# Rotary half turn of two attention stages: from a TensorE matmul to transfers issued by GpSimd, with the cosine product on GpSimd and the softmax-weight step in another place of the order

## The chip, the cores and the metric

The kernel runs on one core of one Trainium2 chip. The metric is the device time of one launch in microseconds (us), the median over runs. TensorE (PE in the profile) does matmuls, VectorE (DVE) and ScalarE (ACT) do element-wise work and can read the matmul result banks (PSUM), GpSimd (POOL) does element-wise work on SBUF and can issue DMA transfers, and SyncE (SP) issues the transfers of the weights. Each engine runs its own instructions strictly in the order of the program; engines meet only at semaphores.

## The reference

Two transformer-like blocks run one after the other on a 256 x 1024 input in float32, 14 stages in all. Two of these stages (layers 0 and 3 of the second block) are differential attention, called A here. Cut to what matters:

```python
def apply_rope(x, cos, sin):                       # heads of 64 columns, halves of 32
    x1, x2 = jnp.split(x, 2, axis=-1)
    return jnp.concatenate([x1 * c - x2 * s, x2 * c + x1 * s], axis=-1)

def diff_attention(h, w_in, w_out, lam_params, subln_g, cos, sin, layer_idx):
    q, k, v = split(h @ w_in)                      # 1024 + 1024 + 1024 columns
    q, k = apply_rope(q, cos, sin), apply_rope(k, cos, sin)
    p = softmax(mask(q @ k.T * scale))             # 8 heads, each with two components
    wts = p[:, :, 0] - lam * p[:, :, 1]
    o = rms_norm(wts @ v, subln_g) * (1 - lam_init)
    return o @ w_out
```

## The kernel before

Activations lie with their feature on the partitions and the 256 tokens along the row. The weights of all 14 stages come as one stream of 1 MB pieces in a ring of three slots. For every piece SyncE issues the transfer into `w_raw` (line 537), ScalarE rounds it into a high part `w_hi` (`hi_ahead`, line 625), VectorE subtracts to get the low part `w_lo` (`lo_ahead`, line 1262), and TensorE multiplies three times per tile with these parts (lines 2222 to 2224). A float32-accurate product is the sum of the three.

Each A stage has 16 pieces: 12 of the input projection (`in0` to `in11`) and four of the output projection (`D0` to `D3`, each in four quarters). The order of all work in an attention stage is a list of tokens, `ATTENTION["A"]`. Every engine walks the same list and does its own share of a token:

- `inK`: TensorE projects piece K into one of three result banks. ScalarE first makes `w_hi` of piece K+2 and then copies the result of piece K to SBUF (`evacuate`, line 876; the buffer `raw_qk` holds two pairs of tiles). VectorE makes `w_lo` of piece K+2.
- `rotK`: the rotation of one pair of tiles, two tiles of queries or two of keys, 128 partitions x 512 columns. TensorE multiplies the raw tile by the signed permutation `turn` (`turn_pair`, line 2450), which swaps the 32-partition halves of each head and negates one of them, into the bank `MISC`. VectorE (`rotate`) multiplies the raw tile by the cosines (line 1665), the turned one by the sines (line 1668) and adds both (line 1682). Before `rot0` it scales the cosine and sine tables by the token's norm factor (lines 1657, 1658).
- `SU`: the scores of head U. TensorE (`scores`, lines 2484, 2485, 2489); then VectorE takes the row maxima (`masked`, lines 1734, 1743), then ScalarE the exponentials (`exponentials`, line 916).
- `NU`: VectorE turns the exponentials of head U into weights (`weights`, lines 1753, 1764, 1767, 1771).
- `TU`: TensorE transposes these weights (line 2559), ScalarE copies them out (line 926).
- `WU`: TensorE multiplies them with the values (`weigh`, lines 2535, 2536), ScalarE copies the result (line 882).

The scores of heads 0 and 1 need rotations 0 and 1, those of heads 2 and 3 need rotations 2 and 3, and so on. Scores of head U also wait for the exponentials of head U-1, since they use the same banks. The first part of the list before, on which every engine's order depends, is:

```
in0 in1 in2 rot0 in3 rot1 in4 S0 rot2 in5 S1 rot3 N0 in6 S2 T0 rot4 N1 in7 W0 S3 T1 rot5 N2 in8 W1 S4 T2 rot6
N3 in9 W2 S5 T3 rot7 N4 sq0 in10 W3 S6 T4 sum0 N5 ...
```

GpSimd builds masks at the start (line 588 ends that), issues 128 transfers of 512 KB for the modulation of the first block (line 595), which end with the mLSTM stage, and has one copy per head in the B stage (line 607). In the A stages it does nothing. Stage C has rotations too (`rot0` to `rot4`), by the same `turn` matmul.

Of the kernel before, what the change touches and what calls it, by code (L numbers as in the profile page):

```python
# [55 lines left out]
for _name, _rows in ROWS:  # L56
# [17 lines left out]
ATTENTION = {  # L74
    "A": """in0 in1 in2 rot0 in3 rot1 in4 S0 rot2 in5 S1 rot3 N0 in6 S2 T0 rot4 N1 in7 W0 S3 T1 rot5 N2 in8 W1 S4 T2 rot6
            N3 in9 W2 S5 T3 rot7 N4 sq0 in10 W3 S6 T4 sum0 N5 ln0 nrm0 sq1 in11 T5 sum1 W4 S7 N6 ln1 D0.0 W5 sq2 hi0 D0.1
            nrm1 T6 N7 D0.2 D0.3 lo0 sum2 W6 ln2 D1.0 D1.1 nrm2 T7 D1.2 D1.3 hi1 lo1 W7 sq3 D2.0 D2.1 sum3 ln3 nrm3
# [88 lines left out]
def build(nc, a, out, stages):  # L166
# [13 lines left out]
    with ExitStack() as ctx:  # L180
# [120 lines left out]
        x_loaded = sem("x_loaded")  # L301
        first_loaded = [sem(f"first_loaded{s}") for s in range(KT)]
        first_mod = sem("first_mod")
        x_scaled = sem("x_scaled")
        xr_T = sem("xr_T")
        c_rows_loaded = sem("c_rows_loaded")
# [3 lines left out]
        cols_ready = sem("cols_ready")  # L310
        xin_T = sem("xin_T")
        ada_loaded = [sem(f"ada_loaded{x}") for x in range(2)]
# [83 lines left out]
        nb_ready = sem("nb_ready")  # L396
        sph_ready = sem("sph_ready")
        spl_ready = sem("spl_ready")
# [107 lines left out]
        def _(sp):  # L506
# [3 lines left out]
            def first(kt):  # L510
                if kt >= FIRST_SLOTS:
                    sp.wait_ge(first_used, 2 * (kt - FIRST_SLOTS) + 2)
                sp.dma_start(first_w[:, kt % FIRST_SLOTS, :, :], a["first"][kt]).then_inc(first_loaded[kt], 16)

# [35 lines left out]
        def _(pool):  # L550
# [46 lines left out]

            for st in plan.steps:
                if st["key"][0] == "B":
                    for kind, u in sequence("B"):  # L600
                        if kind != "U":
                            continue
                        if u < 8:
                            pool.wait_ge(sp_ready, u + 1)
                            if u:
                                pool.wait_ge(r_ready, u)
                            pool.tensor_copy(sp_hi, sp).then_inc(sph_ready, 1)


        @block.scalar  # L610
        def _(act):
# [79 lines left out]
            def opening():  # L691
# [18 lines left out]
                for j in range(4):  # L710
                    act.wait_ge(xin_T, j + 1)
                    act.activation(xt_pair(j), PS[4 + j][:, :].rearrange("p (t n) -> p t n", t=2),
                                   ACT.Copy).then_inc(xt_ready, 2)
                for kt in range(KT):
                    if kt == KT - 2:
                        hi_ahead(2)
                    act.wait_ge(xr_T, kt // 2 + 1)
# [3 lines left out]
                    act.wait_ge(xin_T, 4)  # L721
                    act.activation(work[:, kt, :], acc(kt), ACT.Identity, bias=shift, scale=scale).then_inc(t_ready, 1)
# [521 lines left out]
        def _(dve):  # L1244
# [211 lines left out]
            def opening():  # L1456
# [5 lines left out]
                def total(kt, x):  # L1462
                    dve.wait_ge(first_loaded[kt], 16)
# [186 lines left out]
            def rotate(st, k):  # L1650
# [18 lines left out]
                chained()  # L1669
                if kind == "C":  # L1670
# [23 lines left out]
            def stick_unit(st, u):  # L1694
# [8 lines left out]
                if u < 8:  # L1703
# [14 lines left out]
                    ins.then_inc(nb_ready, 1)  # L1718
                    dve.wait_ge(sph_ready, u + 1)
                    if u:  # L1720
# [498 lines left out]
        def _(pe):  # L2219
# [215 lines left out]

            def turn_pair(st, k, units):

# [5 lines left out]
                if st["rots"] + k:  # L2443
                    pe.wait_ge(roped, st["rots"] + k)
                if kind == "A" and st["att"] + units:
                    pe.wait_ge(ot_ready, st["att"] + units)
                elif kind == "C":
                    pe.wait_ge(ot_ready, st["att"])
                m = MISC[:, 0:nt * T].rearrange("p (t n) -> p t n", t=nt)
# [71 lines left out]
            def weigh(st, u, rots):  # L2521
# [367 lines left out]

            def turn_rows(rows, first, done):  # L2890

                for kt in range(KT):
# [132 lines left out]
```

## Time and profile before

| | before |
|---|---|
| time, median of 3 runs | 2407.66 us (2404.53 to 2410.88) |
| time of the profiled execution | 2406.78 us |
| span of the profiled execution | 2404.7 us |
| TensorE busy | 2345.0 us (98%) |
| VectorE busy | 1718.7 us (71%) |
| ScalarE busy | 1192.0 us (50%) |
| GpSimd busy | 80.7 us (3%) |
| mean granted clock of TensorE | 0.997 |

The span runs from the first to the last instruction; the time of the execution has 2.1 us around it. Busy time is the union of an engine's instructions. The first A stage rotates and scores between 1191 and 1267 us, the second between 2105 and 2181 us. A timeline row gives the start, the busy time, the engine, the line, and in brackets how long the engine had been idle and on whom it waited.

### The profile page before, as it was taken

What the parts mean: (1) busy time and instruction counts of PE and PEld (TensorE: products, weight loads), DVE (VectorE), ACT (ScalarE), POOL (GpSimd) and SP (SyncE); (2) the same over time, 40 slices, a digit from 0 to 9 for tenths busy, and PEclk for the clock granted to TensorE, in tenths of its full rate; (3) what the DMA queues carried; (4) which work ended last, traced back from release to release, by engine and by line L of the source; (5) the groups of instructions that cost most, each with busy time, mean ns of one, the idle gap of its engine ahead of it and who ended that gap; (6) DMA issues with size and microseconds to landing.
All of it is one profiled execution on the core that took longest, in us unless ns stands there. A gap on an engine that the chain in (4) does not pass through costs nothing.

```text
span 2404.7 us, 46561 instructions
## 1 busy us (share of the span) xinstructions
PE 2345.0 (98%) x19290; PEld 2259.5 (94%) x19290; DVE 1718.7 (71%) x2260; ACT 1192.0 (50%) x1489; POOL 80.7 (3%) x163
## 2 busy tenths in 40 slices
PE   6999999999999999999999999999999999999999
PEld 6999988999999989999988999899997899988999
DVE  7888788777877867655677666676667666677665
ACT  5335865334434655433556435654345633546434
POOL 1110000010010000000000000000000000000000
PEclk9999999999999999999999999999999999999999
DMA  8987465787788433455433554436542355443652
GB/s 342 326 314 264 158 217 204 279 295 267 273 297 289 175 135 111 172 194 191 172 123 124 208 192 158 148 116 209 193 175 79 123 204 193 156 153 111 210 192 105
DMA packets 75561, 471.62 MB, mean 196 GB/s; under 512 B 8632, under 2 KB 9144, under 8 KB 26808
## 3 DMA queue, kind: packets, MB, share of 16 engines
q1 hardware_dynamic: 56288, 400.79, 46.5%
q0 software_dynamic: 18432, 67.12, 7.9%
q10 hardware_dynamic: 728, 2.14, 0.3%
q8 instruction: 80, 1.31, 0.2%
q14 instruction: 33, 0.27, 0.0%
HBM read 468.96 MB, written 1.05 MB: 195 GB/s over the span
## 4 chain that ended last, share of the span: by engine, by line
PE 80%; DVE 10%; ACT 4%; DMA 4%; issue 2%; POOL 0%; ACTq 0%; DVEq 0%; POOLq 0%
PE bank L2222 23%; PE bank L2223 23%; PE bank L2224 23%; DVE w_lo L1262 2%; DMA ada_wbuf<-in_ada 2%; PE bank L2228 2%; DVE ada_wbuf L1411 2%; PE bank L2233 2%; PE bank L2229 2%; DMA ARENA<-in_first 1%; ACT w_hi L625 1%; PE bank L2450 1%; PE bank L2484 1%; ACT ARENA L916 0%; DVE ARENA L1734 0%
## 5 line engine op out<-in xcount | busy, mean ns | idle before, releaser
L1262 DVE TENSOR_TENSOR w_lo<-w_raw,w_hi 128x2048 fp32r<-128x2048 f32 x371 | 848.9, 2289 | 319.9 <-ACT w_hi L625 319.1
L625 ACT ACTIVATE w_hi<-w_raw 128x2048 fp32r<-128x2048 f32 x371 | 708.9, 1914 | 508.4 <-PE bank L2224 493.3
L2222 PE MATMUL bank<-h_hi,w_hi 128*128 128x256 f32 x3376 | 944.2, 280 | 1.5 <-DVE w_lo L1262 1.5
L2224 PE MATMUL bank<-h_hi,w_lo 128*128 128x256 f32 x3376 | 935.8, 277 | 0.0
L2223 PE MATMUL bank<-h_lo,w_hi 128*128 128x256 f32 x3376 | 935.8, 277 | 0.0
L2222 PEld LDWEIGHTS bank<-h_hi,w_hi 128*128 128x128 f32 x3376 | 634.7, 188 | 8.3 <-issue 5.1
L2223 PEld LDWEIGHTS bank<-h_lo,w_hi 128*128 128x128 f32 x3376 | 634.8, 188 | 3.5 <-issue 3.3
L2224 PEld LDWEIGHTS bank<-h_hi,w_lo 128*128 128x128 f32 x3376 | 634.6, 188 | 0.0
L2222 PE MATMUL bank<-d_hi,w_hi 128*128 128x256 f32 x1920 | 536.3, 279 | 4.1 <-DVE d_lo L1639 4.0
L2224 PE MATMUL bank<-d_hi,w_lo 128*128 128x256 f32 x1920 | 532.2, 277 | 0.0
L2223 PE MATMUL bank<-d_lo,w_hi 128*128 128x256 f32 x1920 | 532.1, 277 | 0.0
L2222 PEld LDWEIGHTS bank<-d_hi,w_hi 128*128 128x128 f32 x1920 | 360.6, 188 | 7.7 <-DVE d_lo L1639 5.5
L2223 PEld LDWEIGHTS bank<-d_lo,w_hi 128*128 128x128 f32 x1920 | 360.6, 188 | 0.5 <-issue 0.5
L2224 PEld LDWEIGHTS bank<-d_hi,w_lo 128*128 128x128 f32 x1920 | 360.5, 188 | 0.0
L1411 DVE CUSTOM_DVE_ANT_0 ada_wbuf<-ada_wbuf,c_rows 128x1024 f32<-128x1024 f32 x128 | 155.7, 1219 | 31.1 <-DMA ada_wbuf<-in_ada 31.1
L2228 PE MATMUL bank<-h_hi,w_hi 128*128 128x256 f32 x440 | 111.7, 286 | 3.2 <-ACT h_hi L676 2.8
L816 ACT ACTIVATE gate_s<-gate_s 128x512 f32<-128x512 f32 x44 | 27.9, 633 | 170.6 <-DVE gate_s L1572 170.6
L2229 PE MATMUL bank<-h_hi,w_lo 128*128 128x256 f32 x440 | 109.3, 281 | 0.0
L595 POOL DMA_DIRECT2D ada_wbuf<-in_ada x128 | 67.8, 530 | 786.0 <-DVE ada_sum L1411 756.2
L2228 PEld LDWEIGHTS bank<-h_hi,w_hi 128*128 128x128 f32 x440 | 83.5, 190 | 9.4 <-issue 7.7
L789 ACT ACTIVATE gate_s<-bank 128x512 f32<-128x512 f32 x40 | 24.0, 600 | 137.1 <-PE bank L2224 134.8
L1593 DVE CAST d_hi<-hid 128x512 fp32r<-128x512 f32 x88 | 37.5, 426 | 73.8 <-PE bank L2224 73.3
(407 smaller groups left out, 2271.9 us busy)
## 6 DMA issues: line engine op xcount, KB each, us to landing
w_raw<-in_ws SPq DMA_DIRECT2D x371, 1024.0 KB, 4.8
ada_wbuf<-in_ada POOLq DMA_DIRECT2D x128, 512.0 KB, 5.3
ARENA<-in_first SPq DMA_DIRECT2D x8, 1024.0 KB, 19.8
work<-in_x SPq DMA_DIRECT2D x1, 1024.0 KB, 11.3
ARENA<-in_wax ACTq DMA_DIRECT2D x1, 1024.0 KB, 4.8
out_y<-ARENA SPq DMA_DIRECT2D x4, 256.0 KB, 2.2
ARENA<-in_wg ACTq DMA_DIRECT2D x1, 768.0 KB
c_rows<-in_c SPq DMA_DIRECT2D x1, 512.0 KB, 4.9
```

Of the source, the lines that this page charges most:

```text
L595: pool.dma_start(ada_w[:, x, :], a["ada"][2 * (piece - 8) + x]).then_inc(ada_loaded[x], 16)
L625: act.activation(w_hi[:, slot, :], w_raw[:, slot, :], ACT.Copy).then_inc(hi_ready, 1)
L816: act.activation(gate_s[:, :, :], gate_s[:, :, :], ACT.Silu).then_inc(silu_ready, 1)
L1262: dve.tensor_tensor(w_lo[:, s, :], w_raw[:, s, :], w_hi[:, s, :].bitcast(F32), ALU.subtract).then_inc(lo_ready, 1)
L1411: dve.tensor_tensor_reduce(out=w, in0=w, in1=c_rows[:, :], scale=1.0, scalar=0.0, op0=ALU.mult, op1=ALU.add, accum_out=dst).then_inc(ada_c ...
L1593: dve.tensor_copy(d_hi[:, buf, :, :], hid[:, :, :]).then_inc(dve_chain, 1)
L2222: pe.matmul(o, whi, xhi, start=start, stop=False, skip_group_check=True)
L2223: pe.matmul(o, whi, xlo, start=False, stop=False, skip_group_check=True)
L2224: return pe.matmul(o, wlo, xhi, start=False, stop=stop, skip_group_check=True)
L2228: pe.matmul(o, whi, xhi, start=start, stop=False, skip_group_check=True)
L2229: pe.matmul(o, wlo, xhi, start=False, stop=False, skip_group_check=True)
L2233: return pe.matmul(o, whi, xlo, start=False, stop=stop, skip_group_check=True)
```

## The change

In the A stages the half turn of a rotation is no longer a matmul. When ScalarE has copied a pair of tiles to SBUF, GpSimd issues four transfers of 32 partitions x 2 KB, which write the swapped halves into `rot_moved`, a buffer of two places that shares its memory with `sp_r` (of stage B). The sign is put into the scaled sine table with `half_sign`. The product with the cosines moves from VectorE to GpSimd, behind the four transfers of its own rotation and behind the wait for the rotation before it. VectorE waits for the 64 counts of its transfers (`moved`), multiplies by the sines, waits for GpSimd's product (`gpsimd_part`) and adds. Stage C keeps the matmul.

In the list of the A stages, `NU` no longer stands ahead of an `in` token but behind it, ahead of the following `rot`; `rotK` moves behind the next `in`; and `TU` comes ahead of the next `S`.

Several semaphores are merged to make room (`first_loaded` by slot, `xin_T` and `xr_T` into `rows_turned`, `sph_ready` into `gpsimd_part`), and four small memsets fill `half_sign` at the start.

```diff
 ATTENTION = {
-    "A": """in0 in1 in2 rot0 in3 rot1 in4 S0 rot2 in5 S1 rot3 N0 in6 S2 T0 rot4 N1 in7 W0 S3 T1 rot5 N2 in8 W1 S4 T2 rot6
-            N3 in9 W2 S5 T3 rot7 N4 sq0 in10 W3 S6 T4 sum0 N5 ln0 nrm0 sq1 in11 T5 sum1 W4 S7 N6 ln1 D0.0 W5 sq2 hi0 D0.1
+    "A": """in0 in1 in2 rot0 in3 rot1 in4 S0 in5 N0 rot2 S1 in6 T0 rot3 S2 in7 N1 rot4 W0 T1 S3 in8 N2 rot5 W1 T2 S4 in9 N3
+            rot6 W2 T3 S5 in10 N4 rot7 sq0 W3 T4 S6 sum0 N5 ln0 nrm0 sq1 in11 T5 sum1 W4 S7 N6 ln1 D0.0 W5 sq2 hi0 D0.1
...
+        rot_moved = sp_r[:, :, :].rearrange("p a c -> p (a c)")[:, 0:4 * T].bitcast(F32).rearrange(
+            "p (b t n) -> p b t n", b=2, t=2)
+        half_sign = sb("half_sign", [P, 1])
...
+            for q in range(4):
+                link(pool.memset(half_sign[32 * q:32 * q + 32, :], 1.0 if q % 2 else -1.0))
...
             for st in plan.steps:
+                if st["key"][0] == "A":
+                    pool.wait_ge(rope_ready, 3 + st["key"][1])
+                    for k in range(8):
+                        pool.wait_ge(proj_ready, st["evac"] + ROT_PIECE["A"][k] + 1)
+                        for q in range(4):
+                            pool.dma_start(rot_moved[32 * q:32 * q + 32, k % 2, :, :],
+                                           raw_part("A", k)[32 * (q ^ 1):32 * (q ^ 1) + 32, :, :]).then_inc(moved[k % 2], 16)
+                        if st["rots"] + k:
+                            pool.wait_ge(roped, st["rots"] + k)
+                        pool.tensor_tensor(rot_a, raw_part("A", k), cos_r.unsqueeze(1).broadcast_to([P, 2, T]),
+                                           ALU.mult).then_inc(gpsimd_part, 1)
...
-                    link(dve.tensor_tensor(cos_r, cos_t[:, :], rstd[:, :], ALU.mult))
-                    link(dve.tensor_tensor(sin_r, sin_t[:, :], rstd[:, :], ALU.mult))
+                    if kind == "A":
+                        dve.tensor_tensor(cos_r, cos_t[:, :], rstd[:, :], ALU.mult).then_inc(rope_ready, 1)
...
+                        link(dve.scalar_tensor_tensor(out=sin_r, in0=sin_t[:, :], scalar=half_sign[:, 0:1], in1=rstd[:, :],
+                                                      op0=ALU.mult, op1=ALU.mult))
...
-                link(dve.tensor_tensor(rot_a[:, 0:nt, :], raw_part(kind, k)[:, 0:nt, :], cosb, ALU.mult))
-                dve.wait_ge(turned, st["rots"] + k + 1)
-                m = MISC[:, 0:nt * T].rearrange("p (t n) -> p t n", t=nt)
+                if kind != "A":
+                    link(dve.tensor_tensor(rot_a[:, 0:nt, :], raw_part(kind, k)[:, 0:nt, :], cosb, ALU.mult))
+                if kind == "A":
+                    dve.wait_ge(moved[k % 2], 64 * (4 * st["key"][1] + k // 2 + 1))
+                    m = rot_moved[:, k % 2, :, :]
...
                 link(dve.tensor_tensor(rot_b[:, 0:nt, :], m, sinb, ALU.mult))
                 chained()
+                if kind == "A":
+                    dve.wait_ge(gpsimd_part, 16 * st["key"][1] + k + 1)
...
                 if kind == "A":
-                    pe.wait_ge(roped, st["rots"] + rots)
                     if u == 4:
...
                     elif step == "rot":
-                        turn_pair(st, k, outs if kind == "A" else 0)
+                        if kind == "C":
+                            turn_pair(st, k)
                         rots += 1
```

## Rows read from the trace of the kernel before

**Rows 1.** The page, its first part: busy time of each engine

```profile
PE 2345.0 (98%) x19290; PEld 2259.5 (94%) x19290; DVE 1718.7 (71%) x2260; ACT 1192.0 (50%) x1489; POOL 80.7 (3%) x163
```

**Rows 2.** Chain that ended last, 1228 to 1238 us (start, us, what)

```profile
1228.32 0.43 PE bank L2535 x2
1228.75 0.22 PE bank L2536 x2
1228.97 0.64 PE bank L2484 x4
1229.61 0.22 PE bank L2485 x4
1229.83 0.43 PE bank L2489 x2
1230.26 0.33 PE bank L2559 x3
1230.59 0.86 PE bank L2450 x2
...
1237.10 0.43 PE bank L2535 x2
```

**Rows 3.** Line 2450: its matmuls (x42; ns min/median/max, first and last start)

```profile
L2450 PE MATMUL bank<-ARENA,turn x42: 378/592/697, 1191.4 to 2162.3; 128*128 128x512 f32 x40, 128*128 128x256 f32 x2
```

**Rows 4.** Timeline of VectorE, 1205.9 to 1221 us, first A stage

```profile
1205.91 1.15 DVE L1734 TENSOR_REDUCE ARENA<-bank 128x1 f32<-128x256 f32 x4 [2.40 <-PE bank L2489]
...
1210.85 2.29 DVE L1262 TENSOR_TENSOR w_lo<-w_raw,w_hi 128x2048 fp32r<-128x2048 f32 x1 [1.66 <-ACT w_hi L625]
...
1215.58 0.68 DVE L1668 TENSOR_TENSOR ARENA<-bank,hid 128x512 f32<-128x512 f32 x1
...
1216.91 0.17 DVE L1753 RECIPROCAL ARENA<-ARENA 128x4 f32<-128x4 f32 x1
...
1218.65 2.29 DVE L1262 TENSOR_TENSOR w_lo<-w_raw,w_hi 128x2048 fp32r<-128x2048 f32 x1
1221.51 1.15 DVE L1734 TENSOR_REDUCE ARENA<-bank 128x1 f32<-128x256 f32 x4 [0.57 <-PE bank L2489]
```

**Rows 5.** Timeline of ScalarE, 1207 to 1211 us

```profile
1208.89 1.92 ACT L625 ACTIVATE w_hi<-w_raw 128x2048 fp32r<-128x2048 f32 x1
```

**Rows 6.** Timeline of VectorE at the seventh head (S6), first A stage

```profile
1256.60 1.15 DVE L1734 TENSOR_REDUCE ARENA<-bank 128x1 f32<-128x256 f32 x4 [0.59 <-PE bank L2489]
```

**Rows 7.** The same two points (S0, S6) of the second A stage

```profile
2120.02 1.15 DVE L1734 TENSOR_REDUCE ARENA<-bank 128x1 f32<-128x256 f32 x4 [2.41 <-PE bank L2489]
...
2170.52 1.15 DVE L1734 TENSOR_REDUCE ARENA<-bank 128x1 f32<-128x256 f32 x4 [0.60 <-PE bank L2489]
```

**Rows 8.** Timeline of VectorE around rotation 0, first A stage

```profile
1191.35 0.42 DVE L1657 TENSOR_TENSOR hid<-cos_t,rstd 128x256 f32<-128x256 f32 x1
...
1194.07 2.28 DVE L1262 TENSOR_TENSOR w_lo<-w_raw,w_hi 128x2048 fp32r<-128x2048 f32 x1
1196.27 0.69 DVE L1665 TENSOR_TENSOR ARENA<-ARENA,hid 128x512 f32<-128x512 f32 x1
```

**Rows 9.** Timeline of TensorE at rotation 0, first A stage

```profile
1191.38 0.67 PE L2450 MATMUL bank<-ARENA,turn 128*128 128x512 f32 x1 [0.59 <-ACT scrap L839]
```

**Rows 10.** Lines 595 and 607: GpSimd's transfers and its copies

```profile
L595 POOL DMA_DIRECT2D ada_wbuf<-in_ada x128: 527/528/689, 38.1 to 861.9; - x128
...
DMA to landing us min/median/max: 3.6/5.3/8.9
...
L607 POOL CAST sp_r<-ARENA x8: 824/830/840, 1516.2 to 1589.8; 128x768 fp32r<-128x768 f32 x8
```

**Rows 11.** The page, DMA issues (KB each, median us to landing)

```profile
out_y<-ARENA SPq DMA_DIRECT2D x4, 256.0 KB, 2.2
```

**Rows 12.** Windows in stage C: busy time of each engine, granted clock, DMA

```profile
1842.00:1844.00 2.00, 0.00 (x0) 0.00 (x1) 1.97 (x6) 1.93 (x9) 0.00 (x0) 0.98 1.00 426
1844.00:1846.00 2.00, 1.97 (x10) 1.67 (x11) 1.93 (x8) 0.00 (x0) 0.00 (x0) 0.50 0.03 8
1846.00:1848.00 2.00, 2.00 (x14) 1.44 (x12) 1.93 (x9) 1.87 (x10) 0.00 (x0) 0.66 0.00 0
```

**Rows 13.** Timeline of VectorE at the start of the kernel

```profile
19.00 1.23 DVE L1466 CUSTOM_DVE_ANT_0 ARENA<-ARENA,c_rows 128x1024 f32<-128x1024 f32 x1 [4.60 <-DMA ARENA<-in_first]
```

More of the change, by code:

```diff
@@ L301, in build @@
         x_loaded = sem("x_loaded")
-        first_loaded = [sem(f"first_loaded{s}") for s in range(KT)]
+        first_loaded = [sem(f"first_loaded{s}") for s in range(FIRST_SLOTS)]
         first_mod = sem("first_mod")
         x_scaled = sem("x_scaled")
-        xr_T = sem("xr_T")
         c_rows_loaded = sem("c_rows_loaded")
@@ L310, in build @@
         cols_ready = sem("cols_ready")
-        xin_T = sem("xin_T")
+        rows_turned = sem("rows_turned")
         ada_loaded = [sem(f"ada_loaded{x}") for x in range(2)]
@@ L389, in build @@
         turned = sem("turned")
+        moved = [sem(f"rope_moved{x}") for x in range(2)]
         roped = sem("roped")
@@ L396, in build @@
         nb_ready = sem("nb_ready")
-        sph_ready = sem("sph_ready")
+        gpsimd_part = sem("gpsimd_part")
         spl_ready = sem("spl_ready")
@@ L512, in first @@
                     sp.wait_ge(first_used, 2 * (kt - FIRST_SLOTS) + 2)
-                sp.dma_start(first_w[:, kt % FIRST_SLOTS, :, :], a["first"][kt]).then_inc(first_loaded[kt], 16)
+                sp.dma_start(first_w[:, kt % FIRST_SLOTS, :, :], a["first"][kt]).then_inc(first_loaded[kt % FIRST_SLOTS], 16)
             def weights(n):
@@ L606, in _ @@
                                 pool.wait_ge(r_ready, u)
-                            pool.tensor_copy(sp_hi, sp).then_inc(sph_ready, 1)
+                            pool.tensor_copy(sp_hi, sp).then_inc(gpsimd_part, 1)
         @block.scalar
@@ L710, in opening @@
                 for j in range(4):
-                    act.wait_ge(xin_T, j + 1)
+                    act.wait_ge(rows_turned, j + 1)
                     act.activation(xt_pair(j), PS[4 + j][:, :].rearrange("p (t n) -> p t n", t=2),
@@ L716, in opening @@
                         hi_ahead(2)
-                    act.wait_ge(xr_T, kt // 2 + 1)
+                    act.wait_ge(rows_turned, kt // 2 + 5)
                     act.wait_ge(first_mod, kt + 1)
@@ L720, in opening @@
                     act.activation(h_hi[:, kt, :], acc(kt), ACT.Identity, bias=shift, scale=scale).then_inc(hhi_ready, 1)
-                    act.wait_ge(xin_T, 4)
                     act.activation(work[:, kt, :], acc(kt), ACT.Identity, bias=shift, scale=scale).then_inc(t_ready, 1)
@@ L1462, in total @@
                 def total(kt, x):
-                    dve.wait_ge(first_loaded[kt], 16)
+                    dve.wait_ge(first_loaded[kt % FIRST_SLOTS], 16 * (kt // FIRST_SLOTS + 1))
                     w = first_w[:, kt % FIRST_SLOTS, x, :]
@@ L1656, in rotate @@
                     dve.wait_ge(rstd_ready, st["sq"] + 1)
-                    link(dve.tensor_tensor(cos_r, cos_t[:, :], rstd[:, :], ALU.mult))
-                    link(dve.tensor_tensor(sin_r, sin_t[:, :], rstd[:, :], ALU.mult))
+                    if kind == "A":
+                        dve.tensor_tensor(cos_r, cos_t[:, :], rstd[:, :], ALU.mult).then_inc(rope_ready, 1)
+                    else:
+                        link(dve.tensor_tensor(cos_r, cos_t[:, :], rstd[:, :], ALU.mult))
+                    if kind == "A":
+                        dve.wait_ge(masks_ready, 1)
+                        link(dve.scalar_tensor_tensor(out=sin_r, in0=sin_t[:, :], scalar=half_sign[:, 0:1], in1=rstd[:, :],
+                                                      op0=ALU.mult, op1=ALU.mult))
+                    else:
+                        link(dve.tensor_tensor(sin_r, sin_t[:, :], rstd[:, :], ALU.mult))
                     chained()
@@ L1664, in rotate @@
                 sinb = sin_r.unsqueeze(1).broadcast_to([P, nt, T])
-                link(dve.tensor_tensor(rot_a[:, 0:nt, :], raw_part(kind, k)[:, 0:nt, :], cosb, ALU.mult))
-                dve.wait_ge(turned, st["rots"] + k + 1)
-                m = MISC[:, 0:nt * T].rearrange("p (t n) -> p t n", t=nt)
+                if kind != "A":
[3 more added lines that the diff above has]
+                    m = rot_moved[:, k % 2, :, :]
+                else:
+                    dve.wait_ge(turned, k + 1)
+                    m = MISC[:, 0:nt * T].rearrange("p (t n) -> p t n", t=nt)
                 link(dve.tensor_tensor(rot_b[:, 0:nt, :], m, sinb, ALU.mult))
                 chained()
+                if kind == "A":
+                    dve.wait_ge(gpsimd_part, 16 * st["key"][1] + k + 1)
                 if kind == "C":
@@ L1718, in stick_unit @@
                     ins.then_inc(nb_ready, 1)
-                    dve.wait_ge(sph_ready, u + 1)
+                    dve.wait_ge(gpsimd_part, 8 + u + 1)
                     if u:
@@ L2434, in attention_input, with turn_pair @@
                     value_columns(st)
-            def turn_pair(st, k, units):
+            def turn_pair(st, k):
                 kind = st["key"][0]
@@ L2444, in turn_pair @@
                     pe.wait_ge(roped, st["rots"] + k)
[L2445 to L2448, printed above, removed]
+                pe.wait_ge(ot_ready, st["att"])
                 m = MISC[:, 0:nt * T].rearrange("p (t n) -> p t n", t=nt)
@@ L2888, in _, with turn_rows @@
             pe.wait_ge(cols_ready, ROW_TILES)
-            def turn_rows(rows, first, done):
+            def turn_rows(rows, first):
                 for kt in range(KT):
@@ L2896, in turn_rows @@
                     if kt % 2:
-                        last.then_inc(done, 1)
+                        last.then_inc(rows_turned, 1)
             pe.wait_ge(x_loaded, 16)
-            turn_rows(x_in, 4, xin_T)
+            turn_rows(x_in, 4)
             pe.wait_ge(x_scaled, TB)
-            turn_rows(x_rows, 0, xr_T)
+            turn_rows(x_rows, 0)
             pe.wait_ge(masks_ready, 1)
```

## The prediction, made before the changed kernel ran

> **What bounds the kernel now.** I read the page first. TensorE is busy for 98% of the span [rows 1], so the first guess for any change is: what TensorE no longer does comes off the time. That guess has to be tested where the change acts, so I took the chain of waits for one head in the first A stage [rows 2]. It holds nothing but TensorE: weigh 0.43 + 0.22, scores 0.64 + 0.22 + 0.43 = 1.29, transposes 0.33, the turn 0.86, and then a projection from 1231.45 to 1237.10, which is 5.65. One round of the order is 8.8 us and TensorE never waits in it.
>
> Then I read VectorE's timeline for the same work [rows 4], since the order list is walked by every engine. It idles, but its place in the order matters more than its busy time. From the maxima of S0 (1205.91) to the low part of the next piece (1210.85) are 4.94 us, of which 1.66 is a wait for ScalarE. ScalarE starts that high part at 1208.89 [rows 5], directly behind the exponentials of the same head. So there is a chain, maxima, exponentials, high part, low part, with no slack in it: low part k+2 starts 4.94 us after the maxima, whatever TensorE does. Before, this costs nothing, because only a later projection needs that low part, and the weights N were already made ahead of it.
>
> **What is taken off TensorE.** The turn matmuls of line 2450 are 42 records [rows 3], two to a rotation: 21 rotations, of which the five of stage C stay. 16 go, at 0.86 [rows 2]: 13.8 us. TensorE also idled 0.59 us before rotation 0, on a ScalarE copy which only the turn needed [rows 9]; twice that is 1.2. If TensorE stayed the bound, the time would fall by 15.0.
>
> **What the new order does to VectorE.** Its list now reads S3, in8, N2, rot5, S4. N2 is what transpose T2 waits for, and T2 stands ahead of S4 on TensorE. But VectorE gets to N2 only behind the low part of in8, and that ends the chain above. Counted from the start of the maxima of a head:
> - low part starts at 4.94 and gives the engine free 2.20 later (1194.07 to 1196.27) [rows 8]: 7.14
> - N takes 1.74 (1216.91 to 1218.65) [rows 4]: 8.88
> - T 0.33, scores 1.29 [rows 2] and 0.1 for the two hand-overs: maxima of the next head at 10.6.
>
> TensorE meanwhile has a projection and a weigh, 5.65 + 0.65 = 6.3, and waits 2.6. Every second head needs the rotation that stands between N and S as well: sine product and sum take 1.33 (1215.58 to 1216.91) [rows 4] against the 0.33 of T which they cover, so that round is 11.6. The four rounds from S2 to S6 take 10.6 + 11.6 + 10.6 + 11.6 = 44.4. Before they took 1256.60 - 1221.51 = 35.1 [rows 4, 6]. That adds 9.3.
>
> S0 to S2 is a special piece. On VectorE it reads S0, low 7, N0, rot2, S1, low 8, rot3, S2. N0 ends at 8.88, rot2 at 10.2, and only then come the maxima of S1, though TensorE had the scores at 6.9. Low 8 starts at 10.2 + 4.94 = 15.1 and ends at 17.35, rot3 at 18.7, S2 follows, and its maxima are at 20.1. Before it was 1221.51 - 1205.91 = 15.6 [rows 4]: 4.5 more. TensorE has in6 and T0 done at 12.9 and waits 5.8 us for rotation 3.
>
> Ahead of S0 something is won. TensorE enters in3 at 1190.8 instead of 1192.2 and has no second turn, so it reaches S0 2.3 us earlier. VectorE must keep up. The cosines are ready at 1191.8 [rows 8]; four issues at 0.53 [rows 10] start by 1193.4. For the landing of 64 KB between two SBUF places no row exists. Bounds: 2.2 us, a store of 256 KB [rows 11], and 8.9, the slowest of the 512 KB loads of the same queue [rows 10]. I take 3, as these are smaller than the fastest load with 3.6. Rotation 0 then ends at 1197.7, low 5 at 1199.9, rotation 1 at 1201.3, low 6 at 1203.5, just in time for the maxima at 1203.6. With 8.9 it would be 1209.4, which is 3.5 later than before instead of 2.3 earlier. Behind S6 the copy of the transposed weights has moved ahead of the exponentials: 0.4 less.
>
> Sum per A stage: -2.3 + 4.5 + 9.3 - 0.4 = +11.1. The second stage has the same distance from S0 to S6, 50.5 against 50.7 us [rows 4, 6, 7], so twice: +22.2.
>
> **The clock.** New idle time of TensorE is 5.8 once and 2.6 or more four times in each stage. In stage C the trace shows the engine without any matmul from 1842 to 1844 and the granted clock then at 0.50 for two us and 0.66 for the next two, that is at 1.2 instead of 2.4 GHz for some 3.3 us [rows 12]. Whether a fall hurts depends on where it falls: under a projection the wait covers it (6.3 + 1.7 is below 8.9), under T and S it lies on the chain and costs up to 0.33 + 1.29 = 1.6. Bounds per stage: 0, and 1.3 + 4 x 1.6 = 7.8. Between them I take half, 3.9, as the idle ends right before T and S but not each such pause need bring a fall. Twice: +7.8.
>
> **What lies beside other work.** The cosine product on GpSimd has no row; the copy of 768 columns takes 0.83 [rows 10], so 512 columns are at least 0.55, and I bound it at 1.4, twice VectorE's 0.69. It starts when the rotation before it is done and is needed at the next one, 8 us or more later, so it is covered; saved on VectorE are 0.61 per rotation that were not on the chain. The two-place buffer, the four transfers of a rotation (2.1 us of issue) and their landing lie in the same gap. DMA issues of the weight stream do not move in SP's queue. The sine table's other form (once per stage, some 0.1), and the waits dropped in `weigh`, cost nothing. The four memsets at the start, some 0.7 together with their waits, delay VectorE ahead of a 4.60 us wait for a transfer [rows 13] and vanish in it; without that cover they would cost 0.7. The merged semaphores count the same events in the same order.
>
> Two engines may still meet at a port. Product 1 starts when rotation 0 is done, which is when VectorE starts low 5; no row shows GpSimd computing beside VectorE there, so the sum holds nothing for it. The Trainium skill, page SBUF — State Buffer, section on the two separate sides, states that a VectorE instruction with two SBUF inputs and a GpSimd instruction that reads SBUF share a pair of ports which one of them holds for its whole length. By that rule product 1 and low 5 run one after the other and rotation 1 comes later by the product, about 1 us a stage, perhaps 2 with product 2 and low 6: 2439 to 2441 instead of 2437. No row before bears on it.
>
> **Rivals.**
> - *TensorE stays the bound.* It would be so if VectorE and ScalarE could run the weights N and the transfers' wait within TensorE's 7.9 us a round. Busy time speaks for it: VectorE has slack on the whole. Against it stand the two in-order engines and the 8.88. It decides if N is ready 6.3 us after the maxima. Time: 2406.8 - 15.0 = 2391.8.
> - *The transfers are the bound.* From the end of one rotation to the next pass product 1.0, the start of the fourth issue 1.6, the landing L and 1.33, so 3.9 + L, against the 8.5 (rotations 2 to 3) and 11.1 that the order leaves. It decides from a landing of about 5 to 7 us. At L = 8.9 each of seven gaps is 12.8: about 10 more behind S0 and 5.8 ahead of it per stage, 2406.8 + 22.2 + 32 = 2461. For it speaks that one GpSimd issue was seen to land after 8.9; against it that these are an eighth of that size and that no HBM is read.
> - *Gain and loss cancel*, by a shorter chain than I count, for which I see no row: within 7 us of 2407.
>
> **How the numbers follow.** The sum is made against the profiled execution, 2406.78 us, which lies 0.9 below the median of the runs, less than their spread: 2406.8 + 22.2 + 7.8 = 2436.8, so 2437. Without any clock fall it is 2429; 2425 if the rotation were also hidden in the two long rounds of each stage (1.0 each); less the 6.4 between the fastest and the slowest run, about 2420. With every fall on the chain it is 2445, and with the slowest landing ahead of S0 alone (5.8 a stage) 2456. Chances: this forecast 0.78, transfers as the bound 0.10, TensorE as the bound 0.09, cancelling 0.03. Range 2420 to 2456, which leaves out the fast rival, the cancelling and most of the transfer rival. A change of under 0.3% (7 us) is about what a measurement of this kernel cannot tell from none. Slower 0.88, same 0.03, faster 0.09.
>
> **What would show it.** After: no line 2450 in the A stages; in VectorE's timeline the order maxima, low part, reciprocal, with 4.94 between the first two and about 10.6 and 11.6 from maxima to maxima; TensorE waiting 2.6 or more for VectorE's line 1771 before each transpose, and about 6 for the sum of rotation 3; VectorE hardly waiting for transfers behind S0; granted clock below 1 in 1200 to 1260. The prediction is wrong if the maxima stand 8 us apart, or if VectorE's waits end on the DMA.

## The result and the profile after

The changed kernel takes 2445.03 us, median of 4 runs (2442.9 to 2448.81), against 2406.84 (2404.53 to 2410.88) for the kernel before: ratio 1.0156 [1.0142, 1.0169], 38 us slower. The forecast was 2437 in 2420 to 2456. The profiled execution took 2444.43 us with a span of 2442.7.

The page, busy time and chain by engine. TensorE's share fell from 98% [rows 1] although it does 32 matmuls less: it waits now. VectorE is 14% of the chain; before it was 10%.

```profile
PE 2349.8 (96%) x19258; PEld 2266.1 (93%) x19258; DVE 1711.6 (70%) x2244; ACT 1193.1 (49%) x1489; POOL 139.1 (6%) x247
...
PE 72%; DVE 14%; ACT 5%; issue 4%; DMA 4%; SPq 0%; POOL 0%; ACTq 0%; DVEq 0%
```

Line numbers have moved: maxima 1764 (before 1734), low part 1277 (1262), N 1783 to 1801 (1753 to 1771), sine product 1696, sum of the rotation 1712, scores 2511 to 2516, transpose T 2585. VectorE's timeline, first A stage (start, busy time, in brackets the idle time before it and what ended it):

```profile
1189.21 0.42 DVE L1673 TENSOR_TENSOR hid<-cos_t,rstd 128x256 f32<-128x256 f32 x1
1189.55 0.48 DVE L1678 SCALAR_TENSOR_TENSOR hid<-sin_t,half_sign,rstd 128x256 f32<-128x256 f32 x1
1196.47 0.69 DVE L1696 TENSOR_TENSOR ARENA<-sp_r,hid 128x512 f32<-128x512 f32 x1 [6.44 <-DMA sp_r<-ARENA]
1197.19 0.69 DVE L1712 TENSOR_TENSOR ARENA<-ARENA 128x512 f32<-128x512 f32 x1
1197.80 2.29 DVE L1277 TENSOR_TENSOR w_lo<-w_raw,w_hi 128x2048 fp32r<-128x2048 f32 x1
1200.01 1.75 DVE L1696 TENSOR_TENSOR ARENA<-sp_r,hid 128x512 f32<-128x512 f32 x1
...
1204.60 1.15 DVE L1764 TENSOR_REDUCE ARENA<-bank 128x1 f32<-128x256 f32 x4
...
1214.83 1.15 DVE L1764 TENSOR_REDUCE ARENA<-bank 128x1 f32<-128x256 f32 x4
...
1225.99 1.15 DVE L1764 TENSOR_REDUCE ARENA<-bank 128x1 f32<-128x256 f32 x4 [2.47 <-PE bank L2516]
...
1236.87 1.15 DVE L1764 TENSOR_REDUCE ARENA<-bank 128x1 f32<-128x256 f32 x4 [0.60 <-PE bank L2516]
1238.05 0.17 DVE L1773 TENSOR_SCALAR ARENA<-ARENA 128x4 f32<-128x4 f32 x1
1241.81 2.29 DVE L1277 TENSOR_TENSOR w_lo<-w_raw,w_hi 128x2048 fp32r<-128x2048 f32 x1 [3.59 <-ACT w_hi L641]
1244.02 0.17 DVE L1783 RECIPROCAL ARENA<-ARENA 128x4 f32<-128x4 f32 x1
...
1246.46 0.69 DVE L1712 TENSOR_TENSOR ARENA<-ARENA 128x512 f32<-128x512 f32 x1
1249.41 1.15 DVE L1764 TENSOR_REDUCE ARENA<-bank 128x1 f32<-128x256 f32 x4 [2.26 <-PE bank L2516]
```

This is the chain of the forecast: from the maxima at 1236.87 (S3) to the low part 4.94 us, of which VectorE idles 3.59 for the high part, then N, then the rotation, then the next maxima after 12.54. Before, the same two maxima (S3 and S4) stood 8.79 apart:

```profile
1230.30 1.15 DVE L1734 TENSOR_REDUCE ARENA<-bank 128x1 f32<-128x256 f32 x4 [1.18 <-PE bank L2489]
1239.09 1.15 DVE L1734 TENSOR_REDUCE ARENA<-bank 128x1 f32<-128x256 f32 x4 [1.17 <-PE bank L2489]
```

TensorE's side: its waits from 1188 to 1310 us (us in total, times, longest), and four rows of its timeline.

```profile
PE bank L2585 <- DVE ARENA L1801: 9.8, 4, 2.8
PE bank L2511 <- DVE ARENA L1712: 9.2, 4, 5.2
```

```profile
1202.54 0.73 PE L2511 MATMUL bank<-ARENA 64*128 64x256 f32 x4 [2.44 <-DVE ARENA L1712]
...
1223.57 1.23 PE L2511 MATMUL bank<-ARENA 64*128 64x256 f32 x4 [5.22 <-DVE ARENA L1712]
...
1234.99 0.55 PE L2585 MATMUL bank<-ident,ARENA 128*128 128x128 f32 x3 [2.21 <-DVE ARENA L1801]
1235.47 0.71 PE L2511 MATMUL bank<-ARENA 64*128 64x256 f32 x4
```

It waits 19 us in the stage: for N ahead of T1 to T4 (2.21, 2.74, 2.00 and 2.81), and for the rotation's sum ahead of S0, S2, S4 and S6 (2.44, 5.22, 0.78 and 0.78); in before's rows the score matmuls followed directly [rows 2]. The scores behind the long wait take 1.23 instead of 0.71. The windows say why (busy time and instruction count of PE, PEld, DVE, ACT, POOL, then the granted clock, the DMA share and GB/s):

```profile
1203.00:1205.00 2.00, 2.00 (x14) 1.76 (x11) 2.00 (x3) 0.00 (x0) 1.98 (x2) 0.53 0.95 369
1205.00:1207.00 2.00, 2.00 (x13) 2.00 (x12) 0.92 (x5) 1.01 (x5) 0.83 (x1) 0.62 0.60 152
1207.00:1208.00 1.00, 1.00 (x11) 1.00 (x10) 0.00 (x0) 1.00 (x6) 0.00 (x0) 1.00 1.05 442
...
1223.00:1224.00 1.00, 0.43 (x2) 0.43 (x4) 0.51 (x1) 0.00 (x0) 0.40 (x1) 0.79 1.17 164
1224.00:1226.00 2.00, 2.00 (x12) 1.61 (x11) 0.01 (x1) 0.00 (x0) 0.86 (x1) 0.50 0.80 336
...
1234.00:1236.00 2.00, 1.01 (x7) 0.82 (x9) 1.93 (x5) 0.42 (x1) 1.05 (x3) 1.00 0.92 193
```

After the waits of 2.44 and 5.22 us the engine runs at half clock (1.2 GHz) for some three us. After the 2.21 ahead of T1 it does not, nor after the 2.00 ahead of T3. Windows of 1 us show four such falls in each A stage: from 1203, 1223, 1247 and 1271, and at the same places of the second, where the one at S2 begins inside the long wait, at 2155, and lasts some seven us.

GpSimd's timeline ahead of S0, and the transfers' line (durations in ns, minimum/median/maximum):

```profile
1189.92 1.99 POOL L609 DMA_DIRECT2D sp_r<-ARENA  x4 [329.56 <-DVE hid L1673]
1191.93 1.30 POOL L613 TENSOR_TENSOR ARENA<-ARENA,hid 128x512 f32<-128x512 f32 x1
1193.17 2.00 POOL L609 DMA_DIRECT2D sp_r<-ARENA  x4
1197.97 3.24 POOL L613 TENSOR_TENSOR ARENA<-ARENA,hid 128x512 f32<-128x512 f32 x1 [2.80 <-DVE ARENA L1712]
```

```profile
L609 POOL DMA_DIRECT2D sp_r<-ARENA x64: 496/502/532, 1189.9 to 2193.3; - x64
...
DMA to landing us min/median/max: 1.8/4.8/6.3
```

The four issues end at 1191.9 and rotation 0 begins at 1196.47. VectorE stands still for 6.44 us. Queued behind it are low 5 (the low part of piece 5), rotation 1, which the scores of S0 need, and low 6, behind which the maxima of S0 stand. Product 1 (GpSimd's, of rotation 1) takes 3.24 beside low 5 instead of 1.30, and then sine product 1 takes 1.75 instead of 0.69.

Where the 38 us are, in us. A stage is counted from the instruction that makes `rstd` to the same of the next stage; maxima mark the heads. (The column without clock falls is e5 below.)

| part of an A stage | before | after | difference | e5 minus before | forecast |
|---|---|---|---|---|---|
| `rstd` to S0, first / second stage | 19.03 / 19.00 | 19.86 / 19.73 | +0.8 / +0.7 | +0.5 / +0.8 | -2.3 |
| S0 to S2 | 15.60 / 15.61 | 21.39 / 21.38 | +5.8 / +5.8 | +4.8 / +4.8 | +4.5 |
| S2 to S6 | 35.09 / 34.89 | 46.41 / 46.22 | +11.3 / +11.3 | +10.2 / +10.4 | +9.3 |
| S6 to the end | 41.03 / 40.94 | 41.87 / 42.06 | +0.8 / +1.1 | -0.2 / -0.2 | -0.4 |
| clock falls | | in the rows above | | 0 | +3.9 |
| stage | 110.75 / 110.44 | 129.53 / 129.39 | +18.8 / +18.95 | +15.1 / +15.7 | +15.0 |

Outside the two stages 2.1 us are won ahead of the first and 2.2 lost between them. I have no explanation for either that a run tests. Neither need be an effect of the change: the first `rstd` stands at 1186.88 before and 1184.74 after, and e1 to e5 and e8 to e12 spread from 1182.17 to 1190.47.

### The profile page after: what moved, and what is told of

It reads as the page before. It is cut to its first block, busy times and chain, and to the rows that moved or that the text cites. A ratio compares the mean times of both kernels' runs of the same rounds, so it can differ in the third digit from the quotient of the medians.

```text
span 2442.7 us, 46564 instructions
## 1 busy us (share of the span) xinstructions
PE 2349.8 (96%) x19258; PEld 2266.1 (93%) x19258; DVE 1711.6 (70%) x2244; ACT 1193.1 (49%) x1489; POOL 139.1 (6%) x247
## 4 chain that ended last, share of the span: by engine, by line
PE 72%; DVE 14%; ACT 5%; issue 4%; DMA 4%; SPq 0%; POOL 0%; ACTq 0%; DVEq 0%
PE bank L2252 21%; PE bank L2253 20%; PE bank L2254 20%; DVE w_lo L1277 4%; DMA ada_wbuf<-in_ada 3%; ACT w_hi L641 2%; DVE ada_wbuf L1426 2%; PE bank L2263 2%; PE bank L2258 1%; PE bank L2259 1%; ACT ARENA L931 1%; DVE ARENA L1764 1%; DMA ARENA<-in_first 1%; PE bank L2511 0%; DVE ARENA L1481 0%
## 5 line engine op out<-in xcount | busy, mean ns | idle before, releaser
L1426 DVE CUSTOM_DVE_ANT_0 ada_wbuf<-ada_wbuf,c_rows 128x1024 f32<-128x1024 f32 x128 | 155.8, 1221 | 30.4 <-DMA ada_wbuf<-in_ada 30.3
## 6 DMA issues: line engine op xcount, KB each, us to landing
work<-in_x SPq DMA_DIRECT2D x1, 1024.0 KB, 11.2
```

## Experiments

Theory O: the place of N behind the low part, with in-order engines, makes the loss. Rival T: the transfers and GpSimd's product make it. Rival K: it is the granted clock. Each ratio is to the kernel before.

| kernel | us, median | ratio, 95% interval | A stages, us |
|---|---|---|---|
| e1 order alone | 2450.25 | 1.0166 [1.0144, 1.0189] | 130.98 / 132.25 |
| e2 transfers alone | 2434.26 | 1.0099 [1.0078, 1.0121] | 124.59 / 123.50 |
| e3 N ahead again | 2428.66 | 1.008 [1.0059, 1.0102] | 121.23 / 122.10 |
| e4 no transfers | 2441.18 | 1.013 [1.0109, 1.015] | 126.68 / 126.78 |
| e5 waits filled | 2439.98 | 1.0137 [1.0118, 1.0157] | 125.89 / 126.17 |
| e6 issue on ScalarE, new order | 2418.85 | 1.0041 [1.0021, 1.0061] | |
| e7 as e6, product on VectorE | 2413.36 | 1.0023 [1.0011, 1.0035] | |
| e8 issue on GpSimd, new order | 2410.37 | 1.0014 [1.0003, 1.0025] | 112.16 / 108.98 |
| e9 as e8, issued early | 2402.03 | 0.9979 [0.9965, 0.9993] | 109.89 / 106.20 |
| e11 as e9, product on VectorE | 2403.29 | 0.9982 [0.9971, 0.9993] | 109.50 / 106.52 |
| e10 as e7, issued behind the factor | 2407.25 | 0.9999 [0.999, 1.0008] | 111.22 / 109.44 |
| e12 new order, turn on TensorE | 2429.93 | 1.0092 [1.0078, 1.0106] | 122.76 / 119.86 |

In e6 and e7 `rstd` itself comes later, so their stages can't be read by this measure. The stages are of one profiled execution each, and e8's is its fastest of ten, 2401.64 against a median of 2410.37: its stages stand for less than the median loses.

**e1, order alone.** The kernel before with its matmul and VectorE's product, and the changed list (W ahead of the rotation, since there they share a bank):

```diff
-    "A": """... S0 rot2 in5 S1 rot3 N0 in6 S2 T0 rot4 N1 in7 W0 S3 T1 rot5 N2 in8 W1 S4 ...
+    "A": """... S0 in5 N0 rot2 S1 in6 T0 rot3 S2 in7 N1 W0 rot4 T1 S3 in8 N2 W1 rot5 T2 S4 ...
```

> The kernel before with the new place of the weights N, of the rotations and of T ahead of S; the turn stays a matmul, the cosine product stays on VectorE, and weigh stands ahead of rot. Order theory (N behind the low part makes a chain maxima, exponentials, high part, low part, N, T, S): nearly all of the loss without any transfer. Rounds 10.8 and 12.2 us instead of 8.8, S0 to S2 about 21.3, so +16 us per A stage, 2434 to 2442 in all. Transfer theory (the landings make the loss): 2400 to 2412, since there are none.

Measured 2450.25, all of the loss, with 1.0166 against 1.0156, and 8 us above the range expected. The rounds (from maxima to maxima) are 10.8, 11.6, 11.2, 13.4, 10.9, 12.3 us. No transfer and no GpSimd product is in it, so T is not needed for a loss of this size. But the turn's bank and TensorE's matmuls for it are in it, and e12 will show that with another list they cost 22 us; e8 is free of them.

**e2, transfers alone.** The changed kernel with the list of before.

```diff
-    "A": """... S0 in5 N0 rot2 S1 in6 T0 rot3 S2 in7 N1 rot4 W0 T1 S3 ...
+    "A": """... S0 rot2 in5 S1 rot3 N0 in6 S2 T0 rot4 N1 in7 W0 S3 T1 ...
```

> The changed kernel with the order list of before: transfers and GpSimd product stay, N stands ahead of the low part again. Order theory: the loss goes, since the wait for a landing delays VectorE by a round but not the round itself; rounds 8.0 to 8.8, ahead of S0 +0.8: 2400 to 2416. Transfer theory: the landings now stand closer to the rotations and cost even more than in the changed kernel, 2445 or more.

Measured 2434.26: the expectation missed, and T's half of the story is real in this order. VectorE's timeline of e2, then GpSimd's:

```profile
1218.52 1.77 DVE L1773 TENSOR_SCALAR ARENA<-ARENA 128x4 f32<-128x4 f32 x1
1224.37 0.69 DVE L1696 TENSOR_TENSOR ARENA<-sp_r,hid 128x512 f32<-128x512 f32 x1 [4.08 <-ACT ARENA L891]
...
1228.93 2.29 DVE L1277 TENSOR_TENSOR w_lo<-w_raw,w_hi 128x2048 fp32r<-128x2048 f32 x1
1231.13 1.14 DVE L1764 TENSOR_REDUCE ARENA<-bank 128x1 f32<-128x256 f32 x4
```

```profile
1216.92 2.01 POOL L609 DMA_DIRECT2D sp_r<-ARENA  x4 [6.19 <-ACT ARENA L891]
1218.95 1.30 POOL L613 TENSOR_TENSOR ARENA<-ARENA,hid 128x512 f32<-128x512 f32 x1
```

In before's list rotation 3 stands directly behind S1. GpSimd issues its transfers from 1216.92, and they are in place only at 1224.4. The bracket names ScalarE's copy, but GpSimd had seen a copy of this line done at 1216.92; what VectorE waits for is the landing, 5.4 us behind the end of the last issue (the profile gives these four 5.2 to 5.8 from issue to landing). Behind it N0 and the low part wait. Of VectorE's sine products the profile puts 35.3 us of waits to the DMA in e2, 12.7 in the changed kernel. So the new order hides the transfers, and the place of N, chosen with it, costs more than they did.

**e3, N ahead again.** The changed kernel, every N one place up, ahead of `in`.

```diff
-    "A": """... S0 in5 N0 rot2 S1 in6 T0 rot3 S2 in7 N1 rot4 W0 T1 S3 in8 N2 ...
+    "A": """... S0 in5 rot2 S1 N0 in6 T0 rot3 S2 N1 in7 rot4 W0 T1 S3 N2 in8 ...
```

> The changed kernel with N alone moved ahead of the in token (S0 in5 rot2 S1 N0 in6 T0 rot3 S2 N1 in7 ...). Order theory: T no longer waits; rounds are 8.5 (bound by low part and rotation on VectorE) and 9.9 (scores wait for the rotation behind the low part) instead of 10.9 and 12.3, S0 to S2 18.4: about +5 us per stage against before, 2415 to 2422. Transfer theory: as the changed kernel, 2445.

Measured 2428.66, 7 us above the range expected. Moving N alone takes back 18 of the 38 us (by the ratios). The rest is in the rotations: TensorE waits 11.6 us of the first stage for their sum, which still stands behind the low part and right ahead of the scores. O was too narrow; not N alone, but N and the rotation behind the low part.

**e4, no transfers.** The changed kernel without the 64 transfers and without VectorE's wait for them. This leaves out the half turn: the sine product reads the unturned pair.

```diff
-                        for q in range(4):
-                            pool.dma_start(rot_moved[...], raw_part("A", k)[...]).then_inc(moved[k % 2], 16)
...
-                    dve.wait_ge(moved[k % 2], 64 * (4 * st["key"][1] + k // 2 + 1))
-                    m = rot_moved[:, k % 2, :, :]
+                    m = raw_part(kind, k)
```

> The changed kernel without the 64 transfers: VectorE takes the sine product of the raw tile itself, so the half turn is left out. Order theory: only the part ahead of S0 gets faster, 3 us per stage, and 2438 remains. Transfer theory: most of the loss goes, 2392 to 2410.

Measured 2441.18: without any transfer 31 of the 38 us remain (by the ratio), so the transfers are not the cause of most of it. GpSimd's product is still in it; e8 settles that. S0 now comes 16.7 us behind `rstd` in both stages, 2.3 earlier than before. That is the gain ahead of S0 which I had forecast and which the landing ate.

**e5, waits filled.** The changed kernel with unused 128x256 matmuls in TensorE's waits: ahead of S0 (4), S2 (12) and T1 to T4 (5 each).

```diff
+                    if kind == "A":
+                        for _ in range({("S", 0): 4, ("S", 2): 12, ("T", 1): 5, ...}.get((step, k), 0)):
+                            pe.matmul(PS[3][:, 0:T], ident[:, :], causal[:, 0:T], start=True, stop=True)
```

> The changed kernel with matmuls of no use in TensorE's waits: 4 ahead of S0, 12 ahead of S2, 5 ahead of each of T1 to T4, 0.46 us each, into a bank that nobody reads. If the fallen clock costs what I take it for (half-speed scores at S2, S4, S6: 1.3 + 0.9 + 0.5 and the tail of the stage 1.2), each stage gets 3 to 4 us shorter: 2437 to 2439, granted clock 1 throughout. If the clock costs nothing: 2445 or, by fillers that run over, 2446 to 2448.

Measured 2439.98 at a mean clock of 0.996 (0.992 without). More work, 5 us less time; the stages are 3.6 and 3.2 shorter. K is about a seventh of the loss by the medians and a fifth by the stages, as far as the filling itself costs nothing. With the clock up (no 1 us window from 1196 to 1296 or from 2112 to 2212 is under 0.97) a stage is still 15 us longer than before.

**e6, e7, e8, a new list.** If O holds in this wider form, a list that takes N and the rotations out from behind the low part, or leaves them a projection of time, must take the loss back. In these three N stands ahead of `in`, and so does every second rotation (3, 5, 7), so that no low part delays them:

```diff
-    "A": """... in4 S0 in5 N0 rot2 S1 in6 T0 rot3 S2 in7 N1 rot4 W0 T1 S3 in8 N2 rot5 W1 T2 S4 ...
+    "A": """... in4 S0 in5 rot2 S1 N0 rot3 in6 T0 S2 N1 in7 rot4 W0 T1 S3 N2 rot5 in8 W1 T2 S4 ...
```

e8 is that alone. In e6 ScalarE issues the transfers right behind its copy of the pair, and in e7 the product is on VectorE as well:

```diff
                 act.activation(dst, b, ACT.Copy, scale=0.125 if query else 1.0).then_inc(proj_ready, 1)
+                if kind == "A":
+                    act.wait_ge(proj_ready, st["evac"] + i + 1)
+                    for q in range(4):
+                        act.dma_start(rot_moved[...], dst[...]).then_inc(moved[rot % 2], 16)
```

> Transfers issued by ScalarE right behind its copy of the tile, the cosine product on GpSimd, and an order made for them: N and the odd rotation ahead of the low part, the even rotation behind it. Order theory: TensorE is nearly the bound again, rounds of 7.9, and the 13.8 us of turn matmuls mostly come off: 2392 to 2398. If transfers cost as such (issue time on ScalarE 4 x 0.45 us, landing of 4.8): 2400 to 2415.

> As e6, but the cosine product is back on VectorE and GpSimd has no part in the A stages. VectorE has 0.61 us more per rotation and rounds of 9.1 and 7.2: about 1 us per stage more than e6 if the two engines do not hold each other up; the same or less than e6 if GpSimd's product (1.28 alone, up to 3.24 beside a low part) costs VectorE as much. 2393 to 2400.

> The order of e6 with the transfers issued by GpSimd as in the changed kernel: tells what the issuing engine is worth. A GpSimd issue needs 2.0 us and lands after 4.8, so the odd rotation stands ready 7.3 us behind the projection instead of about 4; it holds the low part up by 2.4 in three rounds: 2403 to 2415. If the issuer doesn't matter: as e6.

Measured 2418.85, 2413.36 and 2410.37. e8 has every transfer and every product of the changed kernel and only another list, and takes back 34 of the 38 us: the loss is the list's, as O says. e6 and e7 miss (2392 to 2398 and 2393 to 2400 were expected), in part because of what else ScalarE has to do. Its timeline in e7:

```profile
1184.95 2.56 ACTq L884 DMA_DIRECT2D sp_r<-ARENA  x4
...
1188.19 2.44 ACTq L884 DMA_DIRECT2D sp_r<-ARENA  x4
1190.73 1.91 ACT L630 ACTIVATE w_hi<-w_raw 128x2048 fp32r<-128x2048 f32 x1 [2.57 <-issue]
1192.55 0.45 ACT L666 ACTIVATE lnb<-bank,eps_c 128x256 f32<-128x256 f32 x1
1193.04 0.42 ACT L668 ACTIVATE rstd<-lnb 128x256 f32<-128x256 f32 x1
```

Eight issues take 5.0 us and stand ahead of the norm factor, on which the cosines wait. From the start of the first pair's copy to `rstd` 8.7 us pass, in e8 3.3: the factor comes some 5 us later.

**e9, e10, e11, the start of the stage.** e8 leaves one wait ahead of S0, 6.07 us of VectorE for the landing. GpSimd issues only once the cosines exist, which only its product needs. e9 issues the first two rotations' transfers ahead of that wait; e11 also puts the product back on VectorE; e10 is e7 with ScalarE's first eight issues behind the norm factor.

```diff
+                    for k in (0, 1):
+                        pool.wait_ge(proj_ready, st["evac"] + ROT_PIECE["A"][k] + 1)
+                        for q in range(4):
+                            pool.dma_start(rot_moved[...], raw_part("A", k)[...]).then_inc(moved[k], 16)
                     pool.wait_ge(rope_ready, 3 + st["key"][1])
```

> As e8 (transfers from GpSimd in the mended order), but GpSimd issues the transfers of rotations 0 and 1 as soon as their pieces are evacuated, ahead of its wait for the cosines and of product 0. In e8's trace the pieces were evacuated by 1180 and the first issue started at 1187.35; VectorE waited 6.07 us for the landing ahead of rotation 0, and TensorE 2.1 us for rotation 1 ahead of S0. If the landing behind the cosines is what still costs time ahead of S0: that VectorE wait is gone or under 1 us, TensorE reaches S0 without a wait, and each A stage is about 2 us shorter, 4 us in all: 2404 to 2408. If e8's remaining loss lies elsewhere (clock, stage C): no change from e8's 2410.

> As e9, but the cosine product is back on VectorE, so that GpSimd only issues transfers. VectorE has 0.6 us more to do in every rotation; on the other side the low part and the sine product no longer meet a GpSimd product (1.75 us instead of 0.69 in e8's trace ahead of S0). If TensorE is the bound behind S0, both hide: within 2 us of e9. If VectorE's chain is the bound, 16 x 0.6 = 10 us slower than e9, less 2 x 1.1 us.

> As e7 (transfers issued by ScalarE, product on VectorE, mended order), but the eight issues of rotations 0 and 1 stand behind the norm factor on ScalarE instead of ahead of it. In e7's trace these eight took 5.0 us between 1184.95 and 1190.63 and the norm factor came at 1193.04. If they were e7's loss ahead of S0: the norm factor comes some 5 us sooner, each stage gets 3 to 6 us shorter, 2402 to 2408. If the issues only move their cost (the first rotation waits for them instead): about e7's 2413.

e9 takes 2402.03, ratio 0.9979 [0.9965, 0.9993]: 5 us faster than the kernel before, and 2 below the range expected. Only e9 and e11 beat it. VectorE's timeline of e9:

```profile
1189.48 0.48 DVE L1683 SCALAR_TENSOR_TENSOR hid<-sin_t,half_sign,rstd 128x256 f32<-128x256 f32 x1
1189.99 1.67 DVE L1701 TENSOR_TENSOR ARENA<-sp_r,hid 128x512 f32<-128x512 f32 x1
...
1201.37 1.15 DVE L1769 TENSOR_REDUCE ARENA<-bank 128x1 f32<-128x256 f32 x4 [1.55 <-PE bank L2521]
```

Rotation 0 follows the sines at once, and S0 comes 16.7 us behind `rstd`, as in e4: ahead of S0 the landing is fully covered. e11 is equal to e9 within the intervals, so the cosine product on GpSimd buys nothing here. e10 comes to 2407.25, 6 us better than e7, as expected. The place of the eight issues is so 6 us of e7's miss; what keeps e10 above the 2393 to 2400 once expected of e7 is open.

**e12, the new list without the transfers.** The kernel before with the list of e8.

```diff
-    "A": """... in4 S0 rot2 in5 S1 rot3 N0 in6 S2 T0 rot4 N1 in7 W0 S3 T1 rot5 N2 in8 W1 S4 ...
+    "A": """... in4 S0 in5 rot2 S1 N0 rot3 in6 T0 S2 N1 in7 rot4 W0 T1 S3 N2 rot5 in8 W1 T2 S4 ...
```

> The kernel before, turn matmul and VectorE product kept, with the mended order of e6 to e9. If that order alone brings something, this is as fast as e8 or e9 (2402 to 2410) and the transfers are worth nothing. If TensorE is the bound in this order as in the order of before, the same matmuls take the same time: 2404 to 2411, no change from before beyond 0.3%, and the 5 us that e9 wins come from the turns taken off TensorE. If the turn, now ahead of the low part, makes TensorE wait for rotations (as it did in e1 for up to 5.4 us): 2415 or more.

Measured 2429.93, the third of the three answers. TensorE's timeline of e12, then VectorE's:

```profile
1234.23 1.19 PE L2535 MATMUL bank<-ARENA 128*128 128x256 f32 x2 [2.83 <-DVE ARENA L1682]
```

```profile
1233.39 0.69 DVE L1682 TENSOR_TENSOR ARENA<-ARENA 128x512 f32<-128x512 f32 x1
```

With the turn in the bank that `weigh` writes, W0 has to wait until VectorE has read the turn. This list is good only because the turn has left the bank, and the list of before only because it has not. So e9's gain is no gain of the list alone.

## Why the prediction was right, and its steps

**What bounds the work** (right). The loss is the in-order chain maxima, exponentials, high part, low part, N. The low part starts 4.94 us after the maxima, as in the forecast, and e8 removes 34 of the 38 us by the list alone. N is ready 8.95 us after the maxima at 1225.99, against 8.88.

**S2 to S6, +9.3** (right, short by 0.9 to 1.1). With the clock held up (e5) the rounds of the first stage are 10.9, 11.75, 10.9, 11.7 against 10.6, 11.6, 10.6, 11.6. The hand-overs are dearer than my 0.1: from the start of the transpose to the maxima 1.88 us in the rows above, against 1.62 + 0.1.

**S0 to S2, +4.5** (right). +4.8 in e5. The forecast wait of 5.8 for rotation 3 is 5.22.

**Behind S6, -0.4** (right in size without the falls, -0.2).

**Ahead of S0, -2.3** (wrong, measured +0.8): the step that failed. Two sizes were off in it. I took the landing as 3 us "as these are smaller than the fastest load with 3.6"; the four of rotation 0 took 4.8 to 5.3, and rotation 0 begins 6.8 us behind the cosines instead of 4.6. Smaller did not mean faster. And the sum held nothing for two engines at a port, where 1.1 us went in sine product 1. The 2.2 and the 1.1 account, within 0.2, for the 3.1 by which the term was wrong. By the Trainium skill, page SBUF — State Buffer, section on the two separate sides, a VectorE instruction with two SBUF inputs and a GpSimd instruction that reads SBUF exclude each other. The trace agrees: product 1 starts at 1197.97 inside low 5 (1197.80 to 1200.09) and lasts 3.24 instead of 1.30, ending at 1201.21, and the sine product that meets it lasts 1.75. e4, without transfers but with the same meeting (sine products of 1.67 and 1.79), still reaches S0 2.3 earlier than before. So the meeting alone is covered there, and the landing is what uncovered it.

**The clock, +3.9 a stage** (right, 3.6 and 3.2 in e5 as the whole difference). The kind was off: I let all pauses count by half. Four falls a stage came, after the pause ahead of S0, and at S2, S4 and S6; none at the 2.21 us ahead of T1 or the 2.00 ahead of T3. Their cost is mostly where half speed meets scores on the chain: the scores at 1223.57 take 1.23 instead of 0.71.

**The hidden work** (mostly right). Behind S0 GpSimd's product (1.28 us, bounds 0.55 to 1.4), issues of 0.50 and landings lie beside other work; e4 shows what they cost in all, 3 us a stage, nearly all ahead of S0. VectorE has only two waits for the DMA, 12.7 us in both stages.

**The rivals.** TensorE as the bound failed on the 6.3 us by which N had to be ready: it took 8.95. The transfers as the bound failed although their landing came close to its threshold of 5: the list left them 8.5 us and more. Its figure for S0 (3.5 later) was a little nearer the measured 0.8 later than mine (2.3 earlier). In before's list, e2, this rival is most of the mechanism.

**The sum.** 18.8 and 18.95 per stage against 15.0, that is 7.7 us in two stages; 3.1 of each stage are the start, 0.9 to 1.1 the hand-overs. These are what separates 2437 from 2445.

What stays open: of 7.5 us per stage that leave TensorE, e9 wins 4.2 in the second stage and 0.9 in the first. In the first, TensorE waits 2.62 us for a rotation's sum ahead of S2 with the half clock behind it; in the second the longest such wait is 1.7. No run separates what the two lose elsewhere.

## What to carry to other kernels

When operations move in a list that all engines walk, count each engine's path through it, not only the busiest engine's: here 14 us of matmuls left TensorE, and each of two stages grew by 18.9 us, most of it because N and the rotations were put behind VectorE's weight preparation. A transfer needs its place ahead of whatever else its queue waits for: issuing two rotations before the wait for the cosines was worth 8 us by the medians from e8 to e9 (4 were expected, and the stages of the two profiled executions differ by 5), and the same issues in ScalarE's queue delayed a factor that everything needed. And an order is tuned to the buffers it runs with: e8's list gains with the early transfers and loses 22 us with the matmul's bank.

## What the hardware showed that I had not expected

- 64 KB between two SBUF places, issued by GpSimd in 0.50 us, landed after 1.8/4.8/6.3 us (minimum, median, maximum), about as long as a 512 KB load of the same queue, 5.3 [rows 10]. That median is no constant: the same 64 transfers from the same queue have 2.6 in e8 and 3.6 in e2, with the same 1.8 as the least. No run separates what sets it. From ScalarE an issue took 0.51 to 1.57 us, median 0.61.
- GpSimd's product slows VectorE's smallest instructions too. In e2 a 128x4 TENSOR_SCALAR lasted 1.77 us instead of 0.17, and it ended at 1220.29 with the product (1220.25). It had begun 0.43 before it, while GpSimd was issuing transfers, but issues alone did not hold such an instruction in the changed kernel: two TENSOR_SCALARs of 128x256 at 1212.22, inside the issues of 1211.99 to 1213.99, took 0.58 together, and 0.55 elsewhere. The product did: the 128x4 one at 1216.01 lasted 0.30 and ended at 1216.31, with the product (1215.00 to 1216.28). Why the one of e2 was held 0.43 us before its product began is open.
- Two pauses of nearly one length had unlike results: the clock fell after 2.44 us ahead of S0 and not after 2.21 ahead of T1. It fell too after the 2.74 and 2.81 ahead of T2 and T4, and not after the 2.00 ahead of T3.
